# Second MLP of a two-layer trunk: both products as seven block products, hidden activations kept in DRAM between two phases

## The reference, cut to what matters

```python
for i in range(DEPTH):                        # DEPTH = 2
    mod = (cond @ mod_w[i] + mod_b[i])[:, None, :]
    shift1, scale1, gate1, shift2, scale2, gate2 = jnp.split(mod, 6, axis=-1)
    h = rms_norm(x, norm1_gain[i]) * (1 + scale1) + shift1
    # layer 0: sliding-window attention; layer 1: chunked gMLP spatial gating
    y = mixer(h)
    x = x + gate1 * y
    h = rms_norm(x, norm2_gain[i]) * (1 + scale2) + shift2
    x = x + gate2 * squared_relu_mlp(h, mlp_w1[i], mlp_w2[i])

def squared_relu_mlp(h, w1, w2):              # h 1024 x 1024, w1 1024 x 4096, w2 4096 x 1024
    return jnp.square(jax.nn.relu(h @ w1)) @ w2
```

## Times and profile before

| what | us |
|---|---|
| three runs | 2306.87, 2307.96, 2309.41 (median 2307.96) |
| span of the profiled execution, from the first to the last instruction | 2306.2 |
| PE busy | 2270.8 (98%) |
| PE weight loads busy | 1812.3 (79%) |
| DVE busy | 1279.7 (55%) |
| POOL busy | 803.4 (35%) |
| ACT busy | 711.8 (31%) |

### The profile page before, as it was taken

How to read it: one execution, slowest core, us unless ns; L and a number is a source line. 1 busy time by engine, 2 the same in 40 slices (tenths; PEclk the granted TensorE clock), 3 DMA queues, 4 the chain that set the end, 5 groups by cost and what they waited for, 6 DMA issues and landing times.

```text
span 2306.2 us, 29119 instructions
## 1 busy us (share of the span) xinstructions
PE 2270.8 (98%) x10252; PEld 1812.3 (79%) x10252; DVE 1279.7 (55%) x1641; ACT 711.8 (31%) x978; POOL 803.4 (35%) x622
## 2 busy tenths in 40 slices
PE   7999999999999999999999999999999999999999
PEld 4786787888888888787888888888788888888887
DVE  8689687565565554564334421456554455545455
ACT  4328433223223222233222211224323323322322
POOL 0124403464454452301221112121154455355355
PEclk7999999999999999999999999999999999999999
DMA  6363521212212313223334221222111111111112
GB/s 259 121 185 88 210 92 70 86 55 82 86 51 83 99 55 101 86 87 119 129 118 133 84 72 46 83 73 91 56 49 43 55 55 40 51 55 45 46 64 92
DMA packets 84299, 201.38 MB, mean 87 GB/s; under 512 B 23937, under 2 KB 29953, under 8 KB 83714
## 3 DMA queue, kind: packets, MB, share of 16 engines
q1 hardware_dynamic: 65826, 139.70, 18.9%
q10 hardware_dynamic: 18400, 60.69, 7.5%
HBM read 182.54 MB, written 16.78 MB: 86 GB/s over the span
## 4 chain that ended last, share of the span: by engine, by line
PE 59%; issue 34%; POOL 5%; DVE 0%; POOLq 0%; ACT 0%
PE pp L1570 36%; PE pp L1894 23%; POOL w_lo L432 4%; POOL pr L446 1%; PE pp L1701 0%; POOL w_lo L473 0%; DVE w_lo L1024 0%; PE pp L1680 0%; POOLq L499 0%; DVE x L1398 0%; PE pp L1710 0%; POOLq L431 0%; DVE c_f L1353 0%; ACT w_hi L742 0%; ACT root L533 0%
## 5 line engine op out<-in xcount | busy, mean ns | idle before, releaser
L432 POOL TENSOR_TENSOR w_lo<-w_raw,w_hi 128x1024 fp32r<-128x1024 f32 x136 | 329.9, 2425 | 1186.8 <-ACT w_hi L518 1186.8
L1570 PE MATMUL pp<-h_hi,w_hi 128*128 128x512 f32 x1824 | 602.7, 400 | 15.5 <-DVE h_lo L1166 6.2
L1570 PE MATMUL pp<-h_lo,w_hi 128*128 128x512 f32 x1824 | 594.6, 396 | 0.0
L1570 PE MATMUL pp<-h_hi,w_lo 128*128 128x512 f32 x1824 | 594.5, 396 | 0.0
L1398 DVE SCALAR_TENSOR_TENSOR x<-pp,mod,x 128x512 f32<-128x512 f32 x392 | 294.4, 751 | 278.0 <-PE pp L1894 278.0
L1570 PEld LDWEIGHTS pp<-h_hi,w_hi 128*128 128x128 f32 x1824 | 339.2, 188 | 105.9 <-DVE h_lo L1052 12.9
L1570 PEld LDWEIGHTS pp<-h_hi,w_lo 128*128 128x128 f32 x1824 | 343.2, 188 | 83.2
L1570 PEld LDWEIGHTS pp<-h_lo,w_hi 128*128 128x128 f32 x1824 | 343.3, 188 | 81.2
L518 ACT ACTIVATE w_hi<-w_raw 128x1024 fp32r<-128x1024 f32 x162 | 171.5, 1058 | 615.2 <-PE pp L1570 448.0
L1894 PE MATMUL pp<-c_hi,w_hi 128*128 128x512 f32 x784 | 310.1, 396 | 0.4 <-DVE x L1398 0.4
L1894 PE MATMUL pp<-c_hi,w_lo 128*128 128x512 f32 x784 | 310.1, 396 | 0.0
(11 more groups left out here) (185 smaller groups left out, 2207.6 us busy)
## 6 DMA issues: line engine op xcount, KB each, us to landing
w_raw<-weights SPq DMA_DIRECT2D x218, 512.0 KB, 3.6
mod_t<-mod_w ACTq DMA_DIRECT2D x64, 512.0 KB, 4.1
mod_first<-mod_w SPq DMA_DIRECT2D x16, 512.0 KB, 15.3
mod_late<-mod_w ACTq DMA_DIRECT2D x2, 4096.0 KB, 23.3
v_dram<-v_out ACTq DMA_DIRECT2D x16, 512.0 KB, 5.5
vf<-v_dram ACTq DMA_DIRECT2D x16, 512.0 KB, 3.3
x<-x_in SPq DMA_DIRECT2D x4, 1024.0 KB, 8.1
qf<-q_dram SPq DMA_DIRECT2D x32, 128.0 KB, 2.5
```

The costliest lines, as they stand in the source:

```text
L432: nc.gpsimd.tensor_tensor(out=w_lo[:, s, :, :], in0=w_raw[:, s, :, :], in1=w_hi[:, s, :, :].bitcast(f32), op=ALU.subtract).then_inc(lo_don ...
L1570: last = T.matmul((pp[s] if tile is None else tile)[:, cs], w[:, s, k, :], r[:, k, cs], start=(k == 0 and w is w_hi and r is hi), stop=(k ...
```

## The change

The second MLP is written anew, in two phases.

**Phase 1: all of the first product.** Pairs 0 and 1 (4 units) stay as they were. The other 14 pairs (28 units), called steps n = 0 to 13, are each a 2 x 2 block problem: 2 units by 2 halves of the tokens, with 1024 input channels as 2 x 512. Each is seven block products of 4 chunks x 3 = 12 matmuls, 84 in place of 96. The activation operands of the seven products are made once (`combine_inputs` on DVE, then `operand_high` on ACT, `operand_low` on DVE) and lie in the place of `h_hi`, `h_lo`, `hid_hi`, `hid_lo`. Partial results that feed several outputs are copied out of PSUM by ACT (`f_copy`) and added by DVE (`add`). Each pair yields seven activation blocks for the second product (4 squares, of which 3 are stored, and 4 differences), 256 KB each, which SP stores into `hid_dram` (`save_pair`).

**Phase 2: all of the second product,** steps n = 14 to 29: four groups of 1024 hidden rows with four steps each. A step is 2 rows of outputs, seven block products of 4 chunks x 3 = 12 matmuls and 7 additions to `x` (`down_step`). Ahead of each group its seven operands (1 MB each, 4 pairs of 256 KB) are loaded from `hid_dram` by DMAs that ACT issues, one after each block product of the step before (`last_of_group`), since an operand lies where the low part of the previous one was. They are split by ACT (`group_operand`, 128 x 2048) and DVE (`operand_low`, 128 x 2048). I call this a **regroup**; there are four, after steps 13, 17, 21 and 25.

**Weights** come as quarters of 256 KB (128 x 512 per partition row). Per step POOL makes 4 sums and 4 low parts, DVE 3 low parts, ACT 7 high parts, with a ring of four slots.

**Also:** in the last `closing` (n = 3) the scaled chunks go to `g_f`, which has 8 slots, and DVE no longer waits for `h_done`; and the output stores wait for the counter `x_ev` alone, no longer behind a wait of SP for the last weights.

Core of the diff:

```diff
+def weight_quad(w, n, t):
+    at = (PRODUCTS * n + t) % QUADS
+    return w[:, at // 2, QUADS * (at % 2):QUADS * (at % 2) + QUADS, :]
 # PE
+def fast_products(n, t):
+    up = n < FAST_UP
+    if t < QUADS:
+        pe.wait_ge(w_low_p, 4 * n + t + 1)
+    else:
+        pe.wait_ge(w_low_v, 3 * n + t - QUADS + 1)
+    if n and last_of_group(n - 1):
+        pe.wait_ge(op_low, len(PREPARED) + PRODUCTS * group_after(n - 1) + t + 1)
...
+    elif t in (2, 3, 4) and up:
+        pe.wait_ge(f_copy, 3 * n + t - 1)
+    elif t == 6 and up:
+        pe.wait_ge(f_sum, 3 * n + 2)
+    elif t in (2, 3, 4, 6):
+        pe.wait_ge(x_ev, PRODUCTS * (n - FAST_UP) + {2: 1, 3: 2, 4: 3, 6: 5}[t])
+    for i in range(QUADS):
+        for w, r in ((high, hi), (high, lo), (low, hi)):
+            last = T.matmul(bank, w[:, i, :], r[:, i, :], ...)
+    last.then_inc(f_mm, 1)
 # DVE
+def up_step(n):
+    for t in range(QUADS, PRODUCTS):
+        weight_low(n, t)
+    dve.wait_ge(f_copy, 3 * n + 3)
+    add(3, banks[1], banks[1], 2)
+    dve.wait_ge(hid_out, 16 * OUTPUTS * j)
...
+    dve.wait_ge(f_relu, relus + 3)
+    squared(j, O_B21, banks[0], rectified[2])
+    last_diff(j)
+def down_step(n):
+    for t in range(PRODUCTS):
...
+        dve.wait_ge(f_mm, PRODUCTS * n + t + 1)
+        V.scalar_tensor_tensor(out=xn, in0=banks[BANK[t]], ...).then_inc(x_ev, 1)
+        if t < 3:
+            weight_low(n, QUADS + t)
+        if last_of_group(n) and t >= 4:
+            operand_low(t - 4)
+        if last_of_group(n - 1) and t < 4:
+            operand_low(t + 3)
+for n in range(FAST_UP):
+    up_step(n)
+    if last_of_group(n):
+        for t in range(3):
+            operand_low(t)
 # ACT
+        if last_of_group(n):
+            b = group_after(n)
+            act.wait_ge(f_mm, PRODUCTS * n + t + 1)
+            act.dma_start(operand(t, "f"), hid_dram[QUADS * b:QUADS * b + QUADS, t]...)
+        if after < PRODUCTS * FAST_PAIRS:
+            weight_high(after // PRODUCTS, after % PRODUCTS)
...
+        if last_of_group(n) and t >= 3:
+            group_operand(group_after(n), t - 3)
+        if n and last_of_group(n - 1) and t < 3:
+            group_operand(group_after(n - 1), t + 4)
 # DVE, closing
-                    if not static(k) or k >= 2:
+                    if n < 3 and (not static(k) or k >= 2):
                         dve.wait_ge(h_done, ...)
-                    sp.wait_ge(d_ev, phase(1, PEELED, 1, 28, 7 * q + event))
+                    sp.wait_ge(x_ev, PRODUCTS * ((MLP_GROUPS - 1) * DOWN_PAIRS + q) + event)
```

More of the change, by code:

```diff
@@ L105, in build @@
         shift_b = sb("shift_b", [P, KC])
+        shift_d = sb("shift_d", [P, QUADS])
         with ExitStack() as first:
             mod_first = sb("mod_first", [P, 2 * KC, S], where=first)
+        with ExitStack() as plain:
+            wide_f = sb("wide_f", [P, 4, KC, S], f32, plain)
+        g_f = wide_f[:, 2, :, :]
         h_hi = sb("h_hi", [P, KC, S], f32r)
@@ new lines, in weight_low, with fast_weights @@
+            def weight_low(n, t):
+                pool.wait_ge(w_high, PRODUCTS * n + t + 1)
+                nc.gpsimd.tensor_tensor(out=weight_quad(w_lo, n, t), in0=weight_source(t),
+                                        in1=weight_quad(w_hi, n, t).bitcast(f32), op=ALU.subtract).then_inc(w_low_p, 1)
+            def fast_weights():
+                first = U_MLP[1] // 2
+                for pair in range(1, PLAIN_PAIRS):
+                    for s in range(2):
+                        split_lo(first + pair, s)
+                for n in range(FAST_PAIRS):
+                    sum_of(n, S_3)
+                    weight_low(n, 0)
+                    for r in (S_1, S_2, S_4):
+                        sum_of(n, r)
+                    for t in range(1, QUADS):
+                        weight_low(n, t)
@@ L730, in _, with down_high @@
             closing(U_WO // 2, 1)
[L732 removed]
+            def down_high(layer, g, h, q, part):
                 if part in (0, 3):
@@ new lines, in down_step @@
+            def down_step(n):
+                d = n - FAST_UP
+                q = d % DOWN_PAIRS
+                banks = product_banks(n)
+                for t in range(PRODUCTS):
+                    m, half = WRITES[t]
+                    xn = x[:, 2 * q + m, columns_of(half)]
+                    if t in AFTER:
+                        dve.wait_ge(x_ev, PRODUCTS * d + AFTER[t])
+                    dve.wait_ge(f_mm, PRODUCTS * n + t + 1)
+                    V.scalar_tensor_tensor(out=xn, in0=banks[BANK[t]], scalar=mod[:, 6 + GATE2, 2 * q + m:2 * q + m + 1],
+                                           in1=xn, op0=ALU.mult, op1=ALU.add).then_inc(x_ev, 1)
+                    if t < 3:
[4 more added lines that the diff above has]
+                        operand_low(t + 3)
@@ new lines, in _ @@
+            combine_inputs()
+            plain_outputs(0, (pp[3], pp[0]), (tmp[:, 0, :], tmp[:, 1, :]))
+            operand_low(1)
+            dve.wait_ge(t_sum, 13)
+            for t in (2, 4, 6):
+                operand_low(t)
+            plain_outputs(1, (pp[1], pp[2]), (tmp[:, 0, :], mod_acc[:, :]))
+            for n in range(FAST_UP):
+                up_step(n)
+                if last_of_group(n):
+                    for t in range(3):
+                        operand_low(t)
+            for n in range(FAST_UP, FAST_PAIRS):
+                down_step(n)
@@ L1995 @@
+            first = U_MLP[1] // 2
+            opening_pair(first, 3, (pp[3], pp[0]))
+            pe.wait_ge(evac[1], first)
+            plain_unit(first + 1, 0, pp[1])
+            plain_unit(first + 1, 1, pp[2])
+            for n in range(FAST_PAIRS):
+                for t in range(PRODUCTS):
+                    fast_products(n, t)
 def kernel(x, c, positions, norm1_gain, norm2_gain, mod_w, mod_b, swa_w_qkv, swa_q_gain, swa_k_gain,
```

470 lines of the change are left out of this document (333 added, 137 removed).

## The result

| kernel | time, median (range) | runs | span of the profiled execution |
|---|---|---|---|
| before | 2308.03 us (2306.87 to 2309.41) | 4 | 2306.2 |
| changed | 2254.76 us (2253.77 to 2256.91) | 4 | 2251.9 |

The ratio is 0.9769, 95% interval 0.9755 to 0.9783: 53 us faster, where 8 were forecast and 2278 was the lower end of the range. The forecast was wrong by more than any of its rivals could explain.

What follows compares the result with a forecast made beforehand. PE was taken to bound the kernel, busy 98% of the span. Span 2306.2 - 42.5 = 2263.7, plus stalls 2.3 + 11.5 + 20.4 = 2297.9; with 1.8 around it 2300 us, own range 2292 to 2308, whole range 2278 to 2312.

Steps and rivals of the forecast that it cites:

- a matmul less is worth 0.2333 us: On PE in the rewritten stretch: each removed matmul saves 0.2333 us, so 168 fewer save 39.2 us.
- Rival E: Whole change: it does not do what it says; excluded by counting block-product matmuls, given no chance.
- stall of the special half group: PE's wait for DVE at the special last half group: gone with that order, 0.6 us saved.
- `closing` (waits of 0.3 us and more, and the lags behind them): In `closing`, DVE no longer waits for a `tmp` slot ahead of 6 scaled chunks: 1.6 us saved.
- tail behind the last addition: After DVE's last addition: only the last store is left to land, 1.1 us gained of 4.3.
- start: From the last chunk's low part to step 0's fifth product: DVE and POOL work nearly fills the time, 2.3 us added.
- first regroup: After step 13: all operand lows stand behind that step's end on DVE, 11.5 us added, bounds 6.2 and 13.7.
- later regroups: Three regroups in phase 2: DVE and POOL work overfills the time, 6.8 us each, 20.4 in all, bounds 0.5 and 9.8.
- the port: DVE instructions with both inputs in SBUF and POOL instructions exclude each other; each meeting costs up to a whole instruction.
- B: Regroups: DVE and POOL hardly exclude each other, 7.7 us of stalls, 2273 us; chance 0.25 with its half-way case, 2286.
- C: Regroups: transfers decide, slower than 2312.6 us if 250 GB/s or less, 2324 us at 230 GB/s; chance 0.12.
- D: Phase 1: each step stalls by 1 us as DVE and POOL meet, 14 us added, 2314 us; chance 0.08.

Runs made afterwards that it cites:

- e2: Changed kernel with its new 32-byte tile `shift_d` allocated last, so streamed operands lie at 96 modulo 128 as before; 2303.62 us.
- e5: Changed kernel with each regroup operand low computed for two of its four rows, PE multiplying those two twice; 2229.13 us.
- e6: Changed kernel with the regroups' operand loads halved, ACT and DVE still processing as many elements; 2246.88 us.
- e9: Changed kernel, last step of phase 1 reordered: two rectifications ahead of a weight high part on ACT, operand lows 0 and 1 among DVE's last squares; 2254.12 us.
- e1: Kernel before with one unused tile of 32 bytes per partition ahead of `h_hi`, putting streamed operands at 0 modulo 128; 2254.06 us.
- e12: Kernel before with an unused tile of 32 bytes per partition between `w_hi` and `w_lo`; low weights at 32, streamed operands at 0 modulo 128; 2299.9 us.

## Why the prediction was wrong

**The step that failed** is the first one, "so a matmul less is worth 0.2333 us", with the sum built on it. It counts the matmuls that go and leaves the pace of the some 10,000 that stay as it was, so a change of that pace was put at nothing without a reason. The change moved their operands by 32 bytes, and they run at 0.2267 (0.2333 again in e2): 50.1 us of the span. Rival E, that the change does not do what it says, was closed by counting products; it should have asked as well what the change does that it does not say. The new tile stood in the diff. Nothing in the profile of before could have given the size, since all its matmuls with `w_hi` and `w_lo` ran at one distance.

**The other steps can be read on e2**, the change at the old placement: forecast 2300 us and 2297.9 of span, measured 2303.6 and 2302.0.

| term | forecast, us | measured in e2, us |
|---|---|---|
| stall of the special half group | -0.6 | -0.6 (gone) |
| `closing` (waits of 0.3 us and more, and the lags behind them) | -1.6 | -1.5 |
| tail behind the last addition | 4.3 to 3.2 | 4.3 to 2.5 |
| start | +2.3 | +1.9 |
| first regroup | +11.5 | +13.4: 9.5 ahead of it, 2.8 of slow restart, 1.1 at the end |
| later regroups | +6.8 each | +7.8 each (336 matmuls in 86.2 us, at 0.2333 they are 78.4) |
| phase 1's steps | 0 | 0.3 (1080 matmuls in 252.31 us) |

With 39.2 us for the removed matmuls these sum to 2302, what e2 has. The start and the port's two bounds held. Of the misses, that of the first regroup (1.9 us) is PE's slow restart after a long wait (2.8 us), which had no term. In the later ones it is not: in e2 it came in the first of them (1.7 us) and not in the other two, and the three cost the same. Their 1.0 us over the forecast lies between its bounds, where 6.8 had been chosen and not derived. The first regroup's build-up was also another than forecast: not seven lows in a row alone, but a late quarter of weights that held up ACT, and through it VectorE's square.

**The port** The earlier trace rows was read rightly. Operand lows of 2048 elements were forecast at 2.3 us, and well over that in company: from 1640 us on the means are 2556 ns over 17 and 2829 ns over 12, and POOL's instructions of 512 elements have 1528 over all 234 (1417 in the form that had 1303 before, 1626 in the low parts of sums), as forecast (over 1.5). The Trainium skill calls the shared ports an exclusive lock, and says of VectorE's two-port modes that the one that issues first holds it for its whole instruction ("SBUF — State Buffer", Who interferes with whom); the 3.33 us row, 1.3 of its own and the rest behind an operand low, agrees for two SBUF inputs.

**Rivals.** B (the port hardly meets, 2273) was nearest in number to the result and is refuted as a mechanism by e5: the stalls are there in full. C (the transfers decide) is refuted in size: the loaded stretches ran at 392 to 404 GB/s in the first regroup and at 365 to 368 in the later ones (16 us each), far over its 250, though e6 gives them up to 7.9 us. D is refuted: there is no gap between step 2 and step 13.

## What to carry to other kernels

When a change adds, drops or resizes a tile, compare the pace of the matmuls in a part that it does not touch before crediting it with anything; if it moved, run the old kernel with the same padding. Here 32 unused bytes gave all of the 53 us, and the work that went into saving 168 matmuls gave 4 us at one placement and none at the other. Where instructions of two engines lengthen each other, as here, moving work into the idle time of one of them gains only if the other is idle too: e9 gained 0.6 us by the order, within the spread of the runs, and e5 25.6 by the amount.

## What the runs showed of the hardware

- A matmul of 128x512 float32 in a train took 0.2267, 0.2289 or 0.2333 us at the same granted clock of 1.00, by the distance modulo 128 between the addresses of its weights and its streamed operand: 0; 64; 32 or 96. Over this kernel it is 2.3% of the time (e1).
- The three kinds of matmul that alternate share it: one third at distance 96 cost 46 of the 54 us, and the start-to-start times that grew are the two ahead of the displaced one's (e12).
- After 9.3 us without a matmul, PE's next nine started 0.42 to 0.56 us apart, at a granted clock of 0.53; in e2 fourteen starts were slow after the same wait. After a gap of 2.4 us the clock fell to 0.58 once and stayed at 1.00 another time, in the same kernel.
- A POOL instruction of 1.3 us that met VectorE's operand low took up to 3.3 us, so that the idle time of one engine, read alone, overstates what can be put into it (e9).
